# Selected and banded attention of a prompt: values and probabilities as high and low parts, masks added by TensorE, scores two units ahead of the products

## What is computed

```python
def slc_attend(q, sel, idx, valid, pos):
    ...
    mask = jnp.repeat(valid, SLC_BLOCK, axis=-1) & (kpos <= pos[None, :, None, None])
    s = jnp.einsum('bqghd,bqgkd->bqghk', q, k) * (HD ** -0.5)
    p = masked_softmax(s, mask[:, :, :, None, :])
    return jnp.einsum('bqghk,bqgkd->bqghd', p, v.astype(F32)).astype(q.dtype)

def win_prompt(q_rot, kv_win):
    ...
    d = qpos[:, :, None] - kpos[:, None, :]
    mask = (d >= 0) & (d <= WINDOW) & (kpos[:, None, :] >= 0)
    s = jnp.einsum('bnqghd,bnkgd->bnghqk', qb, band[..., 0, :]) * (HD ** -0.5)
    p = masked_softmax(s, mask[None, :, None, None])
    o = jnp.einsum('bnghqk,bnkgd->bnqghd', p, band[..., 1, :].astype(F32))

def nsa_merge(gates, o_cmp, o_slc, o_win):
    o = (gates[..., None] * jnp.stack([o_cmp, o_slc, o_win], axis=2).astype(F32)).sum(2)
```

## Time and profile before

| | us |
|---|---|
| median of three runs | 2639.19 |
| lowest, highest | 2632.55, 2641.63 |
| profiled execution | 2640.57 |
| its span | 2639.0 |
| TensorE busy | 2427.7 |
| VectorE busy | 1215.4 |
| ScalarE busy | 814.2 |
| GpSimd busy | 317.8 |

### The profile page before, as it was taken

How to read it: one execution, slowest core, us unless ns; L and a number is a source line. 1 busy time by engine, 2 the same in 40 slices (tenths; PEclk the granted TensorE clock), 3 DMA queues, 4 the chain that set the end, 5 groups by cost and what they waited for, 6 DMA issues and landing times. The chain is left out here.

```text
span 2639.0 us, 40412 instructions
## 1 busy us (share of the span) xinstructions
PE 2427.7 (92%) x15386; PEld 2191.8 (83%) x15386; DVE 1215.4 (46%) x2152; ACT 814.2 (31%) x1787; POOL 317.8 (12%) x568
## 2 busy tenths in 40 slices
PE   6987797999777899968979999999999999999999
PEld 6976687999666788844469999987999999999997
DVE  4457565304547766645541223333433333333334
ACT  5353454444434555412231212121311111111110
POOL 1014221021103322255300000000000000000000
PEclk9997699999988999979889999999999999999999
DMA  4012332331110000076501112230121111111111
GB/s 153 17 33 85 104 115 88 87 110 20 42 34 1 1 1 1 1 176 164 136 25 48 48 49 63 66 106 19 49 65 48 48 49 36 45 49 49 49 33 65
DMA packets 216620, 156.77 MB, mean 59 GB/s; under 512 B 76706, under 2 KB 197589, under 8 KB 216372
## 3 DMA queue, kind: packets, MB, share of 16 engines
q1 hardware_dynamic: 186980, 122.06, 16.3%
q0 software_dynamic: 8096, 18.98, 2.7%
q10 hardware_dynamic: 21360, 13.22, 1.7%
HBM read 142.76 MB, written 15.59 MB: 60 GB/s over the span
## 5 line engine op out<-in xcount | busy, mean ns | idle before, releaser
L177 PE MATMUL ps<-brT_r,ff_wih 128*128 128x344 f32 x1008 | 322.2, 320 | 0.0
L179 PE MATMUL ps<-brT_r,ff_wi_r 128*128 128x344 f32 x1008 | 321.9, 319 | 0.0
L178 PE MATMUL ps<-xnT_r,ff_wih 128*128 128x344 f32 x1008 | 321.6, 319 | 0.0
L3717 ACT ACTIVATE ff_sa<-ps 128x344 f32<-128x344 f32 x66 | 30.2, 458 | 563.4 <-PE ps L179 563.3
L177 PE MATMUL ps<-x_r,mg_wh 128*128 128x344 f32 x576 | 185.0, 321 | 6.8 <-DVE xnT_r L165 6.8
L177 PEld LDWEIGHTS ps<-brT_r,ff_wih 128*128 128x128 f32 x1008 | 189.7, 188 | 1.0
L179 PEld LDWEIGHTS ps<-brT_r,ff_wi_r 128*128 128x128 f32 x1008 | 189.6, 188 | 0.0
L178 PEld LDWEIGHTS ps<-xnT_r,ff_wih 128*128 128x128 f32 x1008 | 189.1, 188 | 0.4
L178 PE MATMUL ps<-xnT_r,mg_wh 128*128 128x344 f32 x576 | 184.4, 320 | 0.0
L3753 DVE TENSOR_TENSOR x<-x,ps 128x512 f32<-128x512 f32 (+1 forms) x198 | 134.9, 686 | 100.9 <-PE ps L179 100.1
L179 PE MATMUL ps<-x_r,mg_w_r 128*128 128x344 f32 x552 | 176.3, 319 | 0.0
(11 more groups left out here) (615 smaller groups left out, 5911.0 us busy)
## 6 DMA issues: line engine op xcount, KB each, us to landing
ff_wi<-in_w_ffn_in SPq DMA_DIRECT2D x42, 512.0 KB, 5.2
mg_w<-in_w_in SPq DMA_DIRECT2D x23, 512.0 KB, 4.2
ff_wo<-in_w_ffn_out SPq DMA_DIRECT2D x11, 1024.0 KB, 4.9
s_pages<-in_cache_kv_slc POOLq DMA_DIRECT2D x128, 64.0 KB, 2.8
s_pages<-in_cache_kv_slc SPq DMA_DIRECT2D x128, 64.0 KB, 2.8
sc_X<-in_cache_kv_cmp SPq DMA_DIRECT2D x56, 128.0 KB
sc_X<-in_cache_kv_cmp POOLq DMA_DIRECT2D x56, 128.0 KB, 2.4
mg_w<-in_w_branch SPq DMA_DIRECT2D x23, 256.0 KB, 4.5
```

What stands on the lines that cost most here:

```text
L177: nc.tensor.matmul(out, wh, xh, start=(first and k == 0), stop=False)
L178: nc.tensor.matmul(out, wh, xl, start=False, stop=False)
L179: ins = nc.tensor.matmul(out, wl, xh, start=False, stop=(last and k == n - 1))
L3717: nc.scalar.activation(sa[:, s % 2, :], ps[:, s % 2, 0:BLK], ACT.Silu).then_inc(silued, 1)
```

## The change

In `stage_turn` the values of both branches are split as well: the high part goes where the keys lay, the low part where the value lay, so that a slice of 128 columns is high and low part side by side. In `stage_slc_win`:
- probabilities are kept in two tiles `pTh` and `pTl` of type FR: ScalarE writes the high part of every item, VectorE the low part. `attend` does two FR products per key block, with `pTh` and with `pTl`; the 128 columns of the result are the products with the two parts of the values.
- the masks, with the sign turned and of type FR, are added in PSUM by products with the identity between the two score products; VectorE's subtractions go.
- `use` keeps both halves in `sums`; after the last unit of a block two additions bring them into `acc`.
- TensorE's step u is scores(u + 2), products(u), attend(u - 1); ScalarE's exponentials(u + 1), copies of u; VectorE's maximum(u + 2), low parts of u, use(u - 1). Scores of a unit still need the exponentials of the unit two before.
- an item is free when its low part is written; small tiles move into unused parts of the queries' tile.

```diff
@@ stage_turn, scalar and vector
+        v_raw, v_hi, v_lo = halves("kvsw")[:, :, :, 1, :], halves("kvswR")[:, :, :, 0, :], halves("kvswR")[:, :, :, 1, :]
...
+                for t in range(0, QT, 4):
+                    ins = high(nc, v_hi[:, t:t + 4], v_raw[:, t:t + 4])
+                ins.then_inc(vhigh, 1)
                 act.wait_ge(hid, 1)
...
+                dve.wait_ge(vhigh, 1)
+                for t in range(0, QT, 4):
+                    ins = low(nc, v_lo[:, t:t + 4], v_raw[:, t:t + 4], v_hi[:, t:t + 4])
@@ stage_slc_win, items
+        def item_up(act, m, u):
+            bank, hi, twin, _ = parts(m, u)
+            act.wait_ge(pturned, m + 1)
+            if twin is not None:
+                nc.scalar.activation(twin, bank, ACT.Copy, scale=-(HD ** -0.5))
+                nc.scalar.activation(hi, bank, ACT.Copy, scale=-(HD ** -0.5)).then_inc(item_high, 1)
                 return
+            if u >= 2:
+                act.wait_ge(attended, u - 1)
+            high(nc, hi, bank).then_inc(item_high, 1)
+
+        def item_down(dve, m, u):
+            bank, hi, twin, lo = parts(m, u)
+            dve.wait_ge(item_high, m + 1)
...
+            low(nc, lo, bank, hi).then_inc(item_low, 1)
@@ tensor
                         nc.tensor.matmul(out, qA[:, i % 2, h, :], kk, start=True, stop=False)
+                        if a == 0 and br == 1 and i >= 4:
+                            nc.tensor.matmul(out[:, 0:P], one[:, :], band[:, :], start=False, stop=False)
+                        if a + n == hi - lo:
+                            nc.tensor.matmul(out[:, (n - 1) * P:n * P], one[:, :], causal[:, :], start=False, stop=False)
                         ins = nc.tensor.matmul(out, qB[:, i % 2, h, :], kk, start=False, stop=True)
...
-                        ins = nc.tensor.matmul(ps[:, 6 + u % 2, 0:P], pT[:, u % 2, b * P:(b + 1) * P],
-                                               kv, start=(b == 0), stop=(b == hi - lo - 1))
+                        for x in (pTh, pTl):
+                            ins = nc.tensor.matmul(ps[:, 6 + u % 2, 0:P], x[:, u % 2, b * P:(b + 1) * P], kv,
+                                                   start=(b == 0 and x is pTh), stop=(b == hi - lo - 1 and x is pTl))
...
-                    if u + 1 < NU:
-                        scores(u + 1)
+                    if u + 2 < NU:
+                        scores(u + 2)
@@ scalar
+                exponentials(0)
+                for u in range(NU):
+                    if u + 1 < NU:
+                        exponentials(u + 1)
                     for m in range(first_item[u], first_item[u + 1]):
-                        keep(nc.scalar, m, u)
+                        item_up(act, m, u)
@@ vector
-                    if br == 1 and i >= 4:
-                        chain.link(dve, nc.vector.tensor_tensor(s[:, 0:P], s[:, 0:P], c("band"), ALU.subtract))
-                    chain.link(dve, nc.vector.tensor_tensor(s[:, n - P:n], s[:, n - P:n], c("causal"),
-                                                            ALU.subtract))
...
+                    if h == H - 1:
+                        dve.wait_ge(used, u + 1)
...
+                        chain.link(dve, nc.vector.tensor_tensor(dst, dst, by_part[:, :, :, 0, :], ALU.add))
+                        nc.vector.tensor_tensor(dst, dst, by_part[:, :, :, 1, :], ALU.add).then_inc(summed, 1)
```

More of the change, by code:

```diff
@@ L1856, in stage_slc_win @@
     first_item.append(len(items))
[L1858 to L1862, removed]
     NU = len(units)
@@ L1870, in stage_slc_win @@
         p_ = st.sb("p", [P, 2, S])
[L1871 to L1874, removed]
+        pTh = st.sb("pTh", [P, 2, S], FR)
+        pTl = st.sb("pTl", [P, 2, S], FR)
+        sums = st.sb("sums", [P, H, P])
+        one, causal, band = (qflat[:, x:x + P] for x in (32 * P, 33 * P, 34 * P))
+        small = A["q"][:, :, :].rearrange("p t n -> p (t n)")
+        mx, sm, f = (small[:, x:x + 4] for x in (35 * P, 35 * P + 4, 35 * P + 8))
@@ L1880, in stage_slc_win, with parts @@
                              "attended", "used", "oturned", "okept"))
+        masks_ready, summed = sem("masks_ready"), sem("summed")
         chain = Chain(sem("step"))
         def wait_kept(eng, m):
[L1885 to L1890, removed]
+            if m:
+                eng.wait_ge(item_low, m)
+        def parts(m, u):
             kind, a, n = items[m]
-            bank = ps[0:HD, 4 + m % 2, :]
@@ L1893, in keep @@
             if kind == "q":
[L1894 to L1906, removed]
@@ L1907, in keep @@
-                return
-            if by_act[m] != (eng is nc.scalar):
-                return
[L1910 to L1917, removed]
+                at = lambda x, rows: x[rows, a % 2, HPG * n:HPG * (n + 1), :].rearrange("p h q -> p (h q)")
@@ new lines, in item_down @@
+        def item_down(dve, m, u):
+            bank, hi, twin, lo = parts(m, u)
+            dve.wait_ge(item_high, m + 1)
+            if twin is not None:
+                if items[m][1] < 2:
+                    dve.wait_ge(zeroed, 1)
+                nc.vector.scalar_tensor_tensor(lo, bank, -(HD ** -0.5), hi.bitcast(F32), ALU.mult,
+                                               ALU.subtract).then_inc(item_low, 1)
+                return
+            low(nc, lo, bank, hi).then_inc(item_low, 1)
@@ L2015, in out, with exponentials @@
                                          ps[:, 7, :].rearrange("p (a q) -> p a q", a=4), ACT.Copy).then_inc(okept, 1)
+                for dst, name, scale in ((one, "ident", 1.0), (causal, "causal", -1.0), (band, "band", -1.0)):
+                    nc.scalar.activation(dst[:, :], c(name), ACT.Copy, scale=scale).then_inc(masks_ready, 1)
                 for m in range(2):
-                    keep(nc.scalar, m, 0)
-                for u in range(NU):
+                    item_up(act, m, 0)
+                def exponentials(u):
                     i, h, br = units[u]
```

44 lines of the change are left out of this document (30 added, 14 removed).

## The result

The changed kernel takes 2656.09 us (median of six, 2653.42 to 2662.19) against 2641.14 for the kernel before (median of six): the ratio is 1.0062 [1.0045, 1.008], slower by about 15 us. The forecast was 2635; the time lies just above the upper end of the range, 2656, and the sign was missed.

What follows compares the result with a forecast made beforehand. Late blocks were taken as bound by TensorE's work, early ones by the ring of scores to copy. Blocks 4 to 7 + 11.6, blocks 0 to 3 - 13.9, values - 2, start + 0.3: - 4.0, so 2635 us, range 2613 to 2656.

Steps and rivals of the forecast that it cites:

- Value products: TensorE, 528 key blocks: 1056 records before and after, price 0.111 to 0.109-0.111 us each; - 2 us.
- rival (A): Short TensorE records cost 0.06 us in long chains too; VectorE then bounds the stage: - 38, 2601 us; chance 0.10.
- Masks: 160 mask records on TensorE at 0.11 us, 17.6 us; 96 of them, 10.6 us, in blocks 4 to 7, unhidden.
- Depth: One unit further ahead: transposes' wait for exponentials goes; blocks 4 to 7 save about 3 plus 2.5 us.
- Blocks 0 to 3 - 13.9: Early blocks, 115.5 us before, come to 101.6: TensorE's work plus small-engine turns, some half clock and output waits.
- Queries' bank: Queries' transposes in blocks 4 to 6 also wait for VectorE's 0.69 us subtraction: + 0.7 each, + 4 us.
- output's bank: Values of a block's second unit wait for a copy behind all pieces of a unit: + about 1 us over four blocks.
- end: After the last sum, two additions of 0.69 us before the output can be turned: + 1.5 us.
- Copies: ScalarE takes all 192 pieces instead of 96, about 37 us more, and stays free, busy 169 of 306 us before.
- the start: Stage start: three mask copies before ScalarE's first piece and one more unit of scores first; + 0.3 us.
- (C): Values wait 0.2 to 0.3 us for VectorE's subtraction in 80 units of blocks 3 to 7: + 20, 2655; 0.20 with (D).
- (D): Every wait stays, only in another place, and masks add 17.6 us: 2657; chance 0.20 together with (C).

Runs made afterwards that it cites:

- plain: The changed kernel with one plain float32 value product per key block, on unsplit probabilities, instead of two reduced-format ones; 2648.0 us, 1.0026 against the kernel before.
- depth alone: The kernel before with only scores and exponentials one unit further ahead; plain float32 values, masks on VectorE; 2618.8 us, ratio 0.9914.
- masks and depth: The kernel before with masks by TensorE and one unit further ahead, without the split parts; 2629.6 us, ratio 0.9951.

## Why the prediction was wrong

The stage by its parts: depth - 22.8, masks + 12.0, parts without the clock + 12.8, clock + 9.6, in all + 11.6.

- **Value products, "-2 us": the step that failed.** The price was right, 0.11 a record in long chains (979.34 to 979.57), and rival (A) with it was wrong. But I costed the format by its records alone and took the clock of the earlier trace rows for granted. The format brought + 9.6 us by the clock (changed against plain: the same count of records, and in blocks 4 to 7 the same pauses). I had named it as the thing that would make me wrong ("if the clock of block 0 and 1 changes much"), with no term and no chance for it, and not for the late blocks at all, where 6.4 of the 9.6 lie.
- **Masks, "0.11 each, 10.6 in blocks 4 to 7": right.** From depth alone to masks and depth the late blocks grow by 9.8, the early ones by 2.2, all of it in blocks 2 and 3. As the sum had it, nothing hides them late; in blocks 0 and 1 TensorE's idle time does.
- **Depth: right early, low late.** "Blocks 0 to 3 - 13.9" was for masks and depth; they gave - 13.0. In the late blocks the exponentials were to give 5.5; they gave 7.5 (187.5 to 180.0).
- **Queries' bank, "+ 4", output's bank, "+ 1", and end, "+ 1.5": right.** The subtraction costs the late blocks 4.3, and the waits of the queries' transposes went from 4.6 to 9.1 us. The four late pauses for the output's bank went from 4.0 to 5.3 us. The two additions are the 1.4 behind the last `use`. What I should have read in the row of the output's bank is that wait itself, which the depth doesn't remove and one moved copy does (- 7.9).
- **Copies, "it stays free": the second miss.** The early blocks were forecast at TensorE's work and a turn of the small engines, with no price for 37 us more of copies and for VectorE's wider work. They cost 7.2 there, 4.5 of it with the subtraction. In block 1 of the plain kernel VectorE is busy 19.80 of 25.57 us and no engine is full; my reading is that the chain from transposes over copy and subtraction to values and sum is what is longer.
- **The sum.** Without the end's 1.5, which this cut leaves out, my sum for the stage was - 5.5; it is + 11.6. Of the 17.1 between them the clock is 9.6, the early blocks 8.1 (- 13.9 forecast, - 5.8 in the plain kernel), the values' - 2 another 2.0; the late blocks (10.1 forecast, 7.9 in the plain kernel) take 2.3 off and the start 0.3.
- **Rivals.** The time is that of (C), 2655, and of (D), 2657, by neither mechanism. (C) wanted values waiting for the subtraction in all 80 units of blocks 3 to 7; there are 11 such waits, and with the output's copy moved ahead 5 of 0.9 us in all are left. (D) wanted the waits of before to stay; the largest, 35.9 us, is gone. The right chance for slower would have come from a rival "the clock", and its place stood in the earlier trace rows, block 0 at 0.65.

The Trainium skill, "TensorE: Matmul & The Clock Gate", section "LDWEIGHTS (loading the stationary operand)", gives 107 ns for a load of 128 columns; the steps of the chain at 979.34, 0.11 to 0.12 us, agree within 0.005 us on the mean. The section "Back-to-back issue gap" of that page gives 81 ns for a sustained pair of load and matmul at 128 columns; this case's traces disagree for these records: 0.111 us in a chain of ten.

## What to carry to other kernels

Cost a change of format by the clock too: put a term and a rival on every stretch that is not already at a steady 1.00 and on every pause, and test them with a kernel that differs in the format alone. Where the weight load sets the price, as at 0.111 us a record here, narrow products in a cheaper format save nothing. When an order is deepened, list the waits that it doesn't touch; moving one copy ahead in its engine's order, for such a wait, gave a third as much as the depth. When stages of two profiles are compared, cut each at its own entry: the entries here differ by up to 3.5 us, which is more than some of the costs read.

## What I had not expected of the hardware

- Two FR records of 128 columns cost the same 0.222 us as one plain float32 product, but the granted clock is another: in block 0 it is 0.81 with plain records and 0.57 with FR ones, and in blocks 5 and 7, with the same pauses, 1.00 and 0.93. It comes back in every order tried: the six kernels with FR value records of 128 columns have 0.55 to 0.57 in block 0, the nine others 0.64 to 0.81. Below 1.00 in blocks 4 to 7 are three of the six and none of the nine.
- Doubling the columns of an FR record from 128 to 256 costs 0.007 us at full clock and brings the clock back (0.81 in block 0, or 0.64 with VectorE's masks, and 1.00 in blocks 4 to 7): more work, less time, 13.4 us of the stage with VectorE's masks. What exactly the chip looks at isn't shown.
- The clock can fall in a block that is 93% busy: at 980.85, 1.8 us behind a pause of 1.3 us, and each of the two late falls of the changed kernel made its block some 3 us longer.
